# A hybrid decoder step: bulk loads and page loads issued later, head norms spread by two rounded products, the softmax loop's inverse taken first

## What is computed

```python
h   = rms_norm(x, g_norm1) * (1 + scale1) + shift1            # scale, shift from silu(c) @ w_ada
q, k, v, qi, ki, wi, u_conv, gates = split(h @ w_in)
q, k = rms_norm(q, g_q), rms_norm(k, g_k)                     # over the 128 columns of each head
iscore[t,s] = sum_h wi[t,h] * relu(qi[t,h] . ki[s] / 8)       # indexer, 8 heads of 64
idx = top_k(iscore)                                           # 64 keys (65 for a sample)
p   = softmax(q . k[idx] / sqrt(128) - slope * dist)          # 8 heads, 2 key/value heads
attn = p @ v[idx]                                             # samples also read cache_k, cache_v by page_table
y   = silu(layer_norm(causal_depthwise_conv(a * sigmoid(g), width 31)))
merged = sigmoid(gA) * (attn @ w_o_attn) + sigmoid(gB) * (y @ w_conv_out)
x   = x + gate1 * (merged @ w_out)
x   = x + gate2 * PEER(h2)        # product-key experts: 16384 rows of u_emb and v_emb, all streamed
```

## Time and profile before

| what | value |
|---|---|
| median of 3 runs | 1246.91 us (1246.56 to 1247.79) |
| profiled execution, its own time | 1244.62 us |
| span of its trace | 1242.8 us |
| TensorE matmul busy | 1205.0 us, 97% of the span |
| VectorE / ScalarE / GpSimd busy | 921.6 / 593.2 / 612.3 us |
| moved by DMA | 273.12 MB, mean 220 GB/s |

### The profile page before, as it was taken

One profiled execution on the slowest core, in us unless ns is written; L12 is line 12 of the kernel. 1 busy time (PEld: TensorE's weight loads), 2 busy tenths in 40 slices (PEclk: granted clock), 3 DMA queues, 4 the chain that ended last, 5 costly groups with the idle time before them and its releaser, 6 DMA issues.

```text
span 1242.8 us, 28224 instructions
## 1 busy us (share of the span) xinstructions
PE 1205.0 (97%) x8845; PEld 1113.0 (90%) x8845; DVE 921.6 (74%) x2255; ACT 593.2 (48%) x1016; POOL 612.3 (49%) x307
## 2 busy tenths in 40 slices
PE   5999999989999999999999999999999999999997
PEld 3888887989979999999999999999888888888886
DVE  4899956966756999859999998000567888888866
ACT  2433444666434445445455555444455555555552
POOL 0565564603746577766666666777203444444100
PEclk9999999999999999999999999999999999999999
DMA  9986564424633456655555555667767898888763
GB/s 356 332 285 203 178 216 179 145 81 154 236 134 130 154 188 207 211 191 183 180 184 179 188 178 184 207 215 240 263 224 292 305 335 308 307 305 307 272 227 125
DMA packets 113995, 273.12 MB, mean 220 GB/s; under 512 B 30928, under 2 KB 54192, under 8 KB 113552
## 3 DMA queue, kind: packets, MB, share of 16 engines
q1 hardware_dynamic: 105920, 248.96, 58.7%
q0 software_dynamic: 6432, 19.71, 4.5%
q10 hardware_dynamic: 1584, 3.68, 0.8%
HBM read 249.30 MB, written 23.00 MB: 219 GB/s over the span
## 4 chain that ended last, share of the span: by engine, by line
PE 88%; SPq 3%; issue 2%; DMA 2%; DVE 2%; POOL 2%; ACT 1%; DVEq 0%; ACTq 0%; POOLq 0%
PE ps L2241 19%; PE ps L2184 11%; PE ps L2191 11%; PE ps L2185 11%; PE ps L2244 10%; PE ps L1845 6%; PE ps L1861 6%; PE ps L1855 6%; PE ps L2220 2%; DMA ring<-in_stream 2%; SPq L562 2%; POOL split L672 1%; PE ps L1949 1%; SPq L556 1%; PE ps L1877 1%
## 5 line engine op out<-in xcount | busy, mean ns | idle before, releaser
L732 POOL TENSOR_TENSOR split<-ring,split 128x1024 fp32r<-128x1024 f32 x128 | 307.6, 2404 | 138.4 <-ACT split L1013 138.4
L1013 ACT ACTIVATE split<-ring 128x1024 fp32r<-128x1024 f32 x256 | 271.6, 1061 | 174.6 <-PE ps L2241 167.9
L672 POOL TENSOR_TENSOR split<-ring,split 128x1024 fp32r<-128x1024 f32 x77 | 188.1, 2446 | 189.8 <-ACT split L832 188.3
L2184 PE MATMUL ps<-h2r,split 128*128 128x288 f32 x1024 | 278.6, 297 | 0.7 <-ACT big L1039 0.5
L2185 PE MATMUL ps<-h2r,split 128*128 128x288 f32 x1024 | 278.8, 296 | 0.0
L2241 PE MATMUL ps<-h2r,split 128*128 128x512 f32 x1024 | 257.4, 392 | 1.4 <-DVE h2r L1691 1.4
L2241 PEld LDWEIGHTS ps<-h2r,split 128*128 128x128 f32 x1024 | 184.2, 189 | 34.5 <-ACT act L1069 1.6
L2184 PEld LDWEIGHTS ps<-h2r,split 128*128 128x128 f32 x1024 | 193.0, 188 | 1.2 <-ACT big L1039 0.8
L2185 PEld LDWEIGHTS ps<-h2r,split 128*128 128x128 f32 x1024 | 192.4, 188 | 0.0
L2191 PE MATMUL ps<-h2r,split 128*128 128x288 f32 x1024 | 156.6, 295 | 0.1
L1697 DVE TENSOR_TENSOR split<-ring,split 128x1024 fp32r<-128x1024 f32 x128 | 156.0, 1219 | 0.0
(11 more groups left out here) (290 smaller groups left out, 1613.9 us busy)
## 6 DMA issues: line engine op xcount, KB each, us to landing
ring<-in_stream SPq DMA_DIRECT2D x371, 512.0 KB, 3.4
act_dram<-act SPq DMA_DIRECT2D x128, 128.0 KB, 1.7
big<-in_stream SPq DMA_DIRECT2D x20, 512.0 KB, 7.9
parts<-act_dram SPq DMA_DIRECT2D x16, 512.0 KB, 4.7
big<-act_dram SPq DMA_DIRECT2D x16, 512.0 KB, 5.3
big<-in_cache_k SPq DMA_DIRECT2D x16, 128.0 KB, 2.7
big<-in_cache_v SPq DMA_DIRECT2D x16, 128.0 KB, 3.3
s_act_dram<-act SPq DMA_DIRECT2D x128, 16.0 KB, 1.5
```

Source lines behind the costliest of these rows:

```text
L672: nc.gpsimd.tensor_tensor(split[:, n % 2, 1], ring[:, POS[CUT[n]] % R, :], split[:, n % 2, 0].bitcast(f32), ALU.subtract).then_inc(lin_lo, 1)
L732: nc.gpsimd.tensor_tensor(split[:, (n + ODD) % 2, 1], ring[:, slot_of(n), :], split[:, (n + ODD) % 2, 0].bitcast(f32), ALU.subtract).then_ ...
L1013: nc.scalar.activation(split[:, (n + ODD) % 2, 0], ring[:, slot_of(n), :], ACT.Copy).then_inc(hi_ready, 1)
L2184: MM(out, u_hi[:, k], h_hi[:, k], start=(k == 0), stop=False)
```

## The change

Four edits. The 16 page loads stand behind positions 25 to 47 of the stream in place of 20 to 43; `v_w`, `dist` and `causal` are issued by GpSimd behind its fourth low part, and `stateT` and `qkg` by ScalarE behind the second conv_g (and the state is copied one tile later). The spread of a head's 1/rms is made by two products of rounded numbers (a rounded row and the rest of it) in place of one product in full fp32, one turn later; for this VectorE copies a 10x10 identity and subtracts once, and ScalarE copies once. In the softmax loop VectorE waits for exp and takes the reciprocal before the low part and `merge_conv`. The samples' steps in that loop stand one or two turns later.

```diff
@@ -162,7 +162,7 @@
 QK = [("k", n) for n in range(KV)] + [("q", n) for n in range(H)]
-QK_AT = 3
+QK_AT = 4
...
@@ -174,7 +174,7 @@
-PAGE_AT = [pos for pos in range(NFIRST * R + R, NRING) if pos - R + 1 not in ADA_AT][:NSEQ * NPAGES]
+PAGE_AT = [pos for pos in range(NFIRST * R + 2 * R, NRING) if pos - R + 1 not in ADA_AT][:NSEQ * NPAGES]
...
@@ -377,6 +377,9 @@
+        qk_parts = rhs_other[:, 0, 0:2 * T].rearrange("p (a t) -> p a t", a=2)
+        qk_place = rhs_other[:, 0, 2 * T:2 * T + len(QK)]
...
@@ -658,11 +663,6 @@
-            pool.wait_ge(mod_turned, 2)
-            pool.dma_start(v_w, a["v_w"]).then_inc(vw_in, 16)
-            for dst, src in ((dist_w, "dist"), (causal_w, "causal")):
-                pool.dma_start(dst, a[src]).then_inc(mask_in, 16)
             def low_tile(n):
...
@@ -688,6 +688,11 @@
+                if n == 3:
+                    pool.dma_start(v_w, a["v_w"]).then_inc(vw_in, 16)
+                    for dst, src in ((dist_w, "dist"), (causal_w, "causal")):
+                        pool.dma_start(dst, a[src]).then_inc(mask_in, 16)
                 for k in {16: (1, 2), 21: (3, 4), 26: (5, 6)}.get(n, ()):
...
@@ -798,8 +803,6 @@
-            for dst, src in ((staged_s, "stateT"), (qkg, "qkg")):
-                eng.dma_start(dst, a[src]).then_inc(conv_in, 16)
...
@@ -859,7 +862,10 @@
-                    if m == 3:
+                    if m == 1:
+                        for dst, src in ((staged_s, "stateT"), (qkg, "qkg")):
+                            eng.dma_start(dst, a[src]).then_inc(conv_in, 16)
+                    if m == 4:
                         eng.wait_ge(conv_in, 32)
...
@@ -908,6 +914,9 @@
                     .then_inc(idx_relu, 1)
+                if n == 1:
+                    eng.wait_ge(qk_rstd, 1)
+                    nc.scalar.activation(qk_parts[0:len(QK), 0], qk_rms[0:len(QK)], ACT.Copy).then_inc(qk_high, 1)
...
@@ -965,15 +974,15 @@
-                if n == 13:
+                if n == 15:
...
-                if n in (2, 4):
-                    g = n // 2 - 1
+                if n in (2, 5):
+                    g = n // 3
                     eng.wait_ge(s_rowmax, g + 1)
...
@@ -1251,6 +1260,8 @@
+            dve.wait_ge(v_done, NT)
+            V.tensor_copy(qk_place[0:len(QK)], ident[0:len(QK), 0:len(QK)]).then_inc(qk_low, 1)
             dve.wait_ge(qk_root, 1)
...
@@ -1275,6 +1286,10 @@
                 ins.then_inc(idx_used, 1)
+                if n == 2:
+                    dve.wait_ge(qk_high, 1)
+                    V.tensor_tensor(qk_parts[0:len(QK), 1], qk_rms[0:len(QK)], qk_parts[0:len(QK), 0].bitcast(f32),
+                                    ALU.subtract).then_inc(qk_low, 1)
                 if QK_AT <= n < QK_AT + len(QK):
...
@@ -1396,6 +1411,9 @@
+                dve.wait_ge(exped, n + 1)
+                V.reciprocal(stat[:, n, 2:3], stat[:, n, 1:2]).then_inc(inverse, 1)
                 if n % 2:
...
@@ -1406,42 +1424,34 @@
                     merge_conv(n // 2 - 2)
-                dve.wait_ge(exped, n + 1)
-                V.reciprocal(stat[:, n, 2:3], stat[:, n, 1:2]).then_inc(inverse, 1)
                 if n >= H + 3:
                     low_rhs(rhs_parts, attn, n - H - 3, 2, TP)
-                if n == 14:
-                    dve.wait_ge(s_attn_hi, 1)
-                    V.tensor_tensor(lo_all[:, :, TP:T], attn[:, :, TP:T], hi_all[:, :, TP:T].bitcast(f32), ALU.subtract)\
-                        .then_inc(s_attn_lo, 1)
-                if n in (1, 3):
-                    g = n // 2
+                if n in (1, 4):
+                    g = n // 4
                     dve.wait_ge(s_rows, g + 1)
...
-                if n == 5:
+                if n == 6:
...
-                if n == 6:
+                if n == 8:
...
-                if n == 8:
+                if n == 10:
...
-                if n == 10:
+                if n == 12:
...
-                if n == 12:
+                if n == 14:
...
@@ -1453,6 +1463,9 @@
+            dve.wait_ge(s_attn_hi, 1)
+            V.tensor_tensor(lo_all[:, :, TP:T], attn[:, :, TP:T], hi_all[:, :, TP:T].bitcast(f32), ALU.subtract)\
+                .then_inc(s_attn_lo, 1)
             merge_conv(KC - 2)
...
@@ -1989,12 +2002,14 @@
-                    pe.wait_ge(qk_rstd, 1)
+                    pe.wait_ge(qk_low, 2)
                     if m >= 2:
...
                         pe.wait_ge(qk_ready, m - 1)
-                    MM(pa[2 + m % 2][:, 0:T], ident[0:len(QK), m:m + 1].to_broadcast([len(QK), P]), qk_rms[0:len(QK)],
-                       start=True, stop=True).then_inc(qk_spread, 1)
+                    place = qk_place[0:len(QK), m:m + 1].to_broadcast([len(QK), P])
+                    for part in range(2):
+                        last = MM(pa[2 + m % 2][:, 0:T], place, qk_parts[0:len(QK), part], start=(part == 0), stop=(part == 1))
+                    last.then_inc(qk_spread, 1)
...
@@ -2083,7 +2098,7 @@
-                if n == 6:
+                if n == 7:
...
@@ -2091,14 +2106,14 @@
-                if n == 8:
+                if n == 9:
...
-                if n == 10:
+                if n == 11:
...
@@ -2113,7 +2128,7 @@
-                if n == 12:
+                if n == 13:
...
```

More of the change, by code:

```diff
@@ L482, in build @@
         qk_rstd = sem("qk_rstd")
+        qk_high = sem("qk_high")
+        qk_low = sem("qk_low")
         qk_spread = sem("qk_spread")
```

## The result

The changed kernel takes 1249.54 us (median of 17 runs, 1247.47 to 1255.09), the kernel before 1246.3 us (17 runs beside them, 1242.41 to 1247.79). The ratio is 1.0032, 95% interval 1.0024 to 1.0040: slower by some 4 us (3.2 between the two medians), where 3.6 us less was forecast. The profiled execution after has a span of 1247.5 us against 1242.8, 4.7 more.

What follows compares the result with a forecast made beforehand. TensorE was taken as the bound (88% of the chain), with the SP queue binding in part of the head. Head 1.6, spreads 1.7 and softmax 0.3 sum to 3.6: 1246.91 - 3.6 = 1243.3 us, range 1240.0 to 1246.6.

Steps and rivals of the forecast that it cites:

- forecast 1.6 faster: Head, loads and pages: gain between 0.5 and 2.8 us, the middle taken.
- 8.1 is 2.3 too much, once: Head: a ring load can take 5.8 us unseen; moved bulk loads make landings up to 8.1, costing 2.3 once.
- The thought that halved this price: Head: the SP queue's lateness hides part of any stall, so 1.6 was taken between 0.5 and 2.8.
- 46.5: Head, SP queue: ring load 43 stands behind 18 ring loads and 12 pages, 8.1 + 38.4 us.
- The upper bound: Head: without the early crowd ring load 43 goes out at 92.0 in place of 94.8, a gain of 2.8 us.
- the rule that I had weighed: Head: loads from different issuers share 16 DMA engines, so later bytes compete later; by it alone 0.5 or less.
- forecast 1.7: Indexer loop: two spreads take 0.6 in place of 1.16 us; three pairs in turns 4 to 9 count.
- swallowed as forecast: Indexer loop, turns 10 and 11: the saving is lost as TensorE's 1.37 us wait for VectorE's sum grows.
- My last rival: Indexer loop: the clock falls one tile earlier, behind the grown wait of 205.07; costs 3.4 us, 1246.7; chance 0.08.
- forecast 0.3 faster: Softmax loop: turn 2's wait returns in turn 3, turn 4 loses 0.4, turn 6 gains 0.7; from -1 to 1.5.
- the slow rival: Softmax loop: VectorE and ScalarE set the pace, turns 4 to 15 lose 6.5 in all, 1250.1 us; chance 0.06.
- Slower had 0.07: Whole kernel: chance of being slower by more than about 0.2% (2.5 us); faster 0.68, within 0.2% 0.25.

Runs made afterwards that it cites:

- the kernel without the bulk part: Changed kernel with values' weights, masks and conv state loaded at their old early place, other edits kept; timed against the kernel before: 1.0006 (0.9994 to 1.0018).
- the kernel with TensorE kept busy: Changed kernel plus eight rounded products into an unread bank in turn 3 of the softmax loop; timed against the kernel before: 1.0031 (1.0019 to 1.0043).
- the first attempt: Kernel before with one page behind every third ring load, spreads in two rounded products and samples' steps later: 0.9982 (0.9972 to 0.9992).
- the merge's experiment: Kernel before with the changed softmax parts, but merge_conv of even turns ahead of the wait for exp: 1.0003 (0.9992 to 1.0014).

## Why the prediction was wrong

**The head: forecast 1.6 faster, measured 2.0 slower in the profile. The step that failed is "8.1 is 2.3 too much, once".** The first half held: the waits at 38 to 46 went, the first triple ended at 45.40 for 45.5, and ring load 25 went out at 45.53. Behind it the crowd made two ring loads late, not one. Load 25 was cut 7.6 us after its issue and load 28 landed after 9.58, where the rows have 8.1. TensorE waited 1.73 and 1.49, and I had not priced the clock, which fell behind the first wait and took 1.49 more. So the crowd costs 4.7 there, not 2.3. A ring load of 8.8 to 11.1 us stands in the chain of every kernel with late bulk loads: with GpSimd's loads alone, with half the pages, with early pages.

The thought that halved this price, that a late queue loses nothing by TensorE being late too, failed with it. The queue itself becomes late, since a ring load waits for a slot that TensorE frees: in the kernel after the load of 59.34 stood ready behind its page from 57.20 on, and went out as TensorE ended its stalled tile at 59.30. Here is the SP queue from ring load 24 to ring load 42, behind 18 ring loads and 12 pages, for which I had 46.5; first the kernel without the bulk part, then the kernel after:

```profile
46.89 0.93 SPq L561 DMA_DIRECT2D ring<-in_stream  x2
...
93.69 0.92 SPq L561 DMA_DIRECT2D ring<-in_stream  x2
```

```profile
44.93 0.93 SPq L561 DMA_DIRECT2D ring<-in_stream  x2
...
94.87 0.91 SPq L561 DMA_DIRECT2D ring<-in_stream  x2
```

Without the late crowd it takes 46.80 (46.28 with the pages alone later), with it 49.94 (50.41 in the kernel with TensorE kept busy). So the rate was right, and the crowd costs the queue some 3 us, more than the 2.8 that were to be won. The upper bound is not refuted by this: an undisturbed queue that starts at 44.93 would reach load 42 at 44.93 + 46.80 = 91.7, by this estimate 2.6 ahead of the earlier trace rows. No run has a head without any crowd, so whether TensorE would follow is not shown. With the crowd early and the pages late the values' product stood at 112.41 and 112.83, within the scatter of the head of the kernel before.

The direction of the rule that I had weighed and then averaged away held: loads from ScalarE, SP and GpSimd share the same DMA engines (the Trainium skill, DMA: Bandwidth & Descriptors, "Issuing engines are not separate DMA queues"), and here the trace agrees, with 6.7 us for a page's keys beside `v_w`, where 2.7 is usual. Neither it nor I had said where the same crowd is cheap. Early and without pages it leaves TensorE idle for 0.9 us (the kernel without the bulk part); early and with pages, in the kernel before, for 0.9 at 34 to 46 and 1.1 at 46 to 66; late for 2.3 to 5.1. Why it is cheaper early, with landings of 8.1 us, was not tried by itself and stays open. The absence of pages may be a part of it: pages put early cost TensorE 1.79 at 42.6 with no bulk load out yet.

**The spreads: forecast 1.7, given back.** A pair takes 0.72, where I had put 0.6, and saves 0.44 in place of 0.56:

```profile
199.12 0.79 PE L2011 MATMUL ps<-y_r 10*128 10x288 f32 x4
199.84 1.32 PE L1858 MATMUL ps<-h2r,split 128*128 128x288 f32 x8
```

Four pairs give the 1.8 us at 199.84, and the fourth is swallowed as forecast, as the wait for VectorE's sum grew to 1.84 for the forecast 1.9. So 1.3 to 1.4 arrive at the sum, not 1.7. Turn 3 gave nothing (a wait of 0.64 for ScalarE stands in place of its spread). Behind it the 64 narrow products took 4.65 for 3.81 in the profile after, as the clock fell inside them, and 0.5 was left at the logits. My last rival, "the clock falls one tile earlier", or something near it, is seen: of the five profiled kernels with the new spreads, four (spreads alone, the kernel after with TensorE kept busy, without the bulk part, the first attempt) have it below 0.95 somewhere at 204 to 208, of the twelve without them three. Where it falls there, a spread kernel needs 43.1 to 44.6 us from sum to logits, and 42.5 in the one where it doesn't. The ratio of the spreads alone, 1.0003 (0.9994 to 1.0012), leaves 0.7 us of gain at most. That the longer wait is the cause was not tested by itself.

**The softmax loop: forecast 0.3 faster.** Its pieces were near: turn 2's wait (0.99) went and 1.25 came in turn 3, where I had put the same length; turn 4's grew by 0.53 (forecast 0.4), shown by the merge's experiment to be the merge behind exp; turn 6's fell from 0.93 to 0.23 (forecast 0.7). The waits sum to 3.5 us, where before they sum to 3.3. Turns 12 to 15 had no new wait, so the slow rival did not come. What was missing is again the clock, 3 us in one profile. (ScalarE's and VectorE's 3.0 and 3.2 are 6.2 for two turns, not 6.1; nothing hangs on it.) Over runs both softmax parts together cost 0.0014, the inverse alone 0.0001, the samples' steps alone -0.0008.

**The clock as a whole.** Within the four sets of runs of the kernel before, time rises by 0.45 to 0.66 us for each 0.001 that the mean clock is lower, within those of the kernel after by 1.0. The clock fell from about 0.9932 to 0.9898, so it goes with 1.5 to 3.4 of the 4 us. That is a correlation, and the same microseconds can be those of the waits. Most falls that I followed sat behind a wait or behind narrow products. Which fall the missing clock of most runs belongs to, and whether it could be had back by itself, stays open, since the kernel that kept the softmax's clock at 1.00 in its profile won nothing, and the kernel without the bulk part has 0.9907 at a ratio of 1.0006. A low mean clock alone does not make a kernel slow here.

**The chances.** Slower had 0.07. The range reached from a head that gives 0.5 to one that gives 2.8, and had no case in which it costs, though the same rows priced a landing at 2.3 too much a load and nothing in them said "once": two such loads cost 4.6 against the 2.8 to be won.

## What to carry to other kernels

What a crowd of transfers costs is read from the idle time of the engine that computes, stretch by stretch, not from landing times: ring loads that land after 8.1 us left TensorE idle for 2.0 us in the kernel before, and moving the bulk loads from there into the pages' stretch cost 3 to 4 us. Count the stream loads issued while the bulk is under way, and price each. A wait that is moved ahead of TensorE's narrow products may cost more than its length (here that was seen in single profiles and not in the medians), so read the granted clock of the profile there, and of all timed runs, before a gain ahead of it is booked. Spacing the small page loads (one behind three stream loads for two) was worth 0.25%, where moving loads later gained at most 0.08%.

## What the runs showed of the hardware

- The clock fell at different places in the seventeen profiles, one of each kernel (windows of 2 us at 26 to 36, 44 to 50, 54 to 72, 202 to 214 and 256 to 274). TensorE does the same work in all of them up to 37 us, and between 26 and 34 the clock fell in eleven and not in six, among them both with and without late bulk loads. Only the fall at the indexer loop's narrow products, between 214 and 230 us by the kernel, stood in all seventeen.
- A 512 KB ring load took 8.8 to 11.1 us to land beside 1.3 to 2.3 MB of bulk loads and the pages (six kernels), where the earlier trace rows have 5.48 later on.
- At the 1.2 GHz level eight rounded products of 288 columns took 2.29 us for 1.32, and 64 narrow products of 16 columns in which it fell 4.65 for 3.81.
- The 128 KB of a page's keys landed after 2.7 us at 60 to 100 us, at a DMA share of 0.88, and after 6.7 us at 45 to 60, at a share of 0.95.
